# Sample attention values in four TensorE column groups: probabilities stationary, cache moving

## The reference

```python
def dilated_gather_decode(q, kv_new, kv_cache, dil, n_keys, slopes):
    ...
    s = (jnp.einsum('bthe,btkhe->bthk', q, kvg[:, :, :, 0]) * (ATT_DH ** -0.5)
         - slopes[:, None] * (dil * kk).astype(jnp.float32)[None, :])
    ...
    o = jnp.einsum('bthk,btkhe->bthe', p, kvg[:, :, :, 1]) / l[..., None]
```

## Time and profile before

| | us |
|---|---|
| median of three runs | 1918.61 |
| lowest and highest run | 1913.48, 1918.93 |
| the profiled execution, its own time | 1915.92 |
| span of the profiled execution | 1914.1 |
| TensorE matmul busy | 1828.6 (96%) |
| VectorE, ScalarE, GpSimd busy | 1039.6, 910.9, 773.9 |
| granted TensorE clock, mean over the span | 0.978 |

### The profile page before, as it was taken

The page is one execution under the profiler, slowest core; times in us unless marked ns, Lnnn a source line. Parts: engine busy times, 40 slices in busy tenths (PEclk is TensorE's granted clock), DMA queues, the critical chain, the costliest instruction groups (busy, mean ns, idle before and its releaser), DMA issues.

```text
span 1914.1 us, 32457 instructions
## 1 busy us (share of the span) xinstructions
PE 1828.6 (96%) x14108; PEld 1761.3 (92%) x14108; DVE 1039.6 (54%) x1120; ACT 910.9 (48%) x1064; POOL 773.9 (40%) x225
## 2 busy tenths in 40 slices
PE   8999999999979999999999979999999999899997
PEld 7999989999969999888989968999999999899997
DVE  4454555675386654455545463776254455557743
ACT  5555555444454435344444443443455565554443
POOL 4545434555215554321221201355354454455541
PEclk9999989999989999999999988999999999899999
DMA  8766854555435555845455522454667668545552
GB/s 269 260 222 245 296 177 154 186 180 166 129 111 172 181 168 187 238 144 160 140 160 141 159 71 68 131 176 161 209 219 265 225 240 289 187 133 176 176 182 84
DMA packets 306036, 346.33 MB, mean 181 GB/s; under 512 B 7847, under 2 KB 269479, under 8 KB 305887
## 3 DMA queue, kind: packets, MB, share of 16 engines
q1 hardware_dynamic: 257968, 260.36, 43.2%
q10 hardware_dynamic: 47927, 83.90, 12.5%
HBM read 299.66 MB, written 44.82 MB: 180 GB/s over the span
## 4 chain that ended last, share of the span: by engine, by line
PE 82%; DVE 9%; ACT 4%; issue 2%; DMA 1%; ACTq 1%; PEldq 0%; DVEq 0%
PE acc L1485 20%; PE acc L1486 20%; PE acc L1492 20%; PE mix L1625 2%; PE mix L1921 2%; PE mix L1883 1%; PE mix L1547 1%; PE acc L1513 1%; ACT w_hi L433 1%; PE acc L1514 1%; DVE w_lo L925 1%; PE acc L1519 1%; PE mix L1856 1%; PE mix L1637 1%; PE mix L1714 1%
## 5 line engine op out<-in xcount | busy, mean ns | idle before, releaser
L1392 POOL TENSOR_TENSOR w_lo<-raw,w_hi 128x2048 fp32r<-128x2048 f32 (+2 forms) x162 | 690.3, 4266 | 712.0 <-ACT w_hi L433 712.0
L1485 PE MATMUL acc<-g_hi,w_hi 128*128 128x264 f32 x2544 | 638.2, 289 | 8.7 <-DVE gate L1182 2.9
L1486 PE MATMUL acc<-g_lo,w_hi 128*128 128x264 f32 x2544 | 627.4, 284 | 0.0
L433 ACT ACTIVATE w_hi<-raw 128x2048 fp32r<-128x2048 f32 (+3 forms) x260 | 455.7, 1755 | 160.7 <-PE acc L1492 79.1
L925 DVE TENSOR_TENSOR w_lo<-raw,w_hi 128x2048 fp32r<-128x2048 f32 (+2 forms) x98 | 381.1, 3888 | 269.0 <-ACT w_hi L433 269.0
L1485 PEld LDWEIGHTS acc<-g_hi,w_hi 128*128 128x128 f32 x2544 | 478.3, 188 | 17.2 <-issue 12.2
L1486 PEld LDWEIGHTS acc<-g_lo,w_hi 128*128 128x128 f32 x2544 | 480.8, 189 | 1.3
L1492 PE MATMUL acc<-g_hi,w_lo 128*128 128x264 f32 x2544 | 343.8, 285 | 0.6 <-POOL w_lo L1392 0.6
L1492 PEld LDWEIGHTS acc<-g_hi,w_lo 128*128 128x128 f32 x2544 | 325.9, 188 | 2.3 <-POOL w_lo L1392 0.8
L1425 POOL TENSOR_TENSOR h_lo<-hid,h_hi 128x528 fp32r<-128x528 f32 x44 | 59.1, 1343 | 332.9 <-ACT h_hi L707 332.9
L1485 PE MATMUL acc<-h_hi,w_hi 128*128 128x264 f32 x664 | 164.1, 284 | 0.0
(11 more groups left out here) (238 smaller groups left out, 2460.1 us busy)
## 6 DMA issues: line engine op xcount, KB each, us to landing
raw<-in_w_ffn_in_dram SPq DMA_DIRECT2D x88, 1024.0 KB, 5.3
raw<-in_w_in_ret_dram SPq DMA_DIRECT2D x48, 1024.0 KB, 7.0
raw<-in_w_in_attn_dram SPq DMA_DIRECT2D x36, 1024.0 KB, 5.6
st<-in_state_ret_dram ACTq DMA_DIRECT2D x64, 512.0 KB, 6.7
out_dram<-st ACTq DMA_DIRECT2D x64, 512.0 KB, 6.2
raw<-in_w_ffn_out_dram SPq DMA_DIRECT2D x32, 768.0 KB, 4.8
raw<-in_w_ffn_out_dram SPq DMA_DIRECT2D x32, 640.0 KB, 4.9
raw<-in_w_out_ret_dram SPq DMA_DIRECT2D x16, 1024.0 KB, 7.5
```

What stands on the lines that cost most here:

```text
L433: A(w_hi[:, u % SPL, 0:size[u]], raw[:, u % RAW, 0:size[u]], ACT.Copy).then_inc(hi_split, 1)
L1392: TT(w_lo[:, u % SPL, 0:size[u]], raw[:, u % RAW, 0:size[u]], w_hi[:, u % SPL, 0:size[u]].bitcast(F32), ALU.subtract).then_inc(lo_by_pool, 1)
L1485: MM(out, wh, x_hi[:, ks[k], :], start=first and k == 0, stop=False)
L1486: MM(out, wh, x_lo[:, ks[k], :], start=False, stop=False)
```

## The change

At s = 7 all matmuls of the quad are done, with the operands swapped: the four columns of probabilities of a sample and block x are stationary (128 x 4) and the 256 values of the quad move (128 x 256). Sample b = 4 half + j goes to column group j of the array (`tile_position=(0, 32*j)`), with its result on PSUM partitions 32j to 32j+3 of bank 2, columns 256 half on. Half 0 is done in slot 0 and half 1 in slot 1. VectorE then copies the whole bank (128 x 512) to `dprod` in SBUF. At s = 8, in slot 0, TensorE turns four 128 x 128 blocks of `dprod` into bank 3, and nothing is done in slot 1. VectorE picks the wanted heads for both tiles with four copies of 64 partitions x 8.

```diff
@@ VectorE, decode_end @@
-                    if s >= 7:
-                        t = s - 7
-                        dve.wait_ge(dpv_done, 2 * q + t + 1)
+                    if s == 7:
+                        dve.wait_ge(dpv_done, 2 * q + 1)
+                        nc.vector.tensor_copy(dprod, mix[:, 2, :].rearrange("p (x n) -> p x n", x=2))\
+                            .then_inc(dpv_read, 1)
+                    if s == 8:
+                        dve.wait_ge(dpv_done, 2 * q + 2)
                         for half in range(2):
                             a = 64 * half
-                            src = mix[a:a + 64, 3, 320 + 32 * t:352 + 32 * t].rearrange("p (b h) -> p b h", h=4)
-                            ins = nc.vector.tensor_copy(y[a:a + 64, 2 * q + t, SEQ:T], src[:, :, 2 * t + half])
+                            src = mix[a:a + 64, 3, :].rearrange("p (g t j r) -> p g t j r", g=2, t=2, j=4)
+                            for t in range(2):
+                                ins = nc.vector.tensor_copy(
+                                    y[a:a + 64, 2 * q + t, SEQ:T].rearrange("p (g j) -> p g j", g=2),
+                                    src[:, :, t, :, 2 * t + half])
                         ins.then_inc(dpv_read, 1)
@@ TensorE, decode @@
-                    if s >= 7:
-                        t = s - 7
+                    if s == 7:
                         pe.wait_ge(dpt_ready, q + 1)
-                        for b in [4 * part + j for part in parts for j in range(4)]:
-                            out = mix[:, 3, 320 + 32 * t + 4 * b:324 + 32 * t + 4 * b]
+                        for half in parts:
                             for x in range(2):
-                                ins = MM(out, vc[:, b, x, t * P:(t + 1) * P], dPT[:, x, 4 * b:4 * b + 4],
-                                         start=(x == 0), stop=(x == 1))
+                                for j in range(4):
+                                    b = 4 * half + j
+                                    ins = MM(mix[32 * j:32 * j + 4, 2, half * UC:(half + 1) * UC],
+                                             dPT[:, x, 4 * b:4 * b + 4], vc[:, b, x, :],
+                                             start=(x == 0), stop=(x == 1), tile_position=(0, 32 * j))
                         if 1 in parts:
                             ins.then_inc(dpv_done, 1)
+                    if s == 8 and 0 in parts:
+                        pe.wait_ge(dpv_read, 2 * q + 1)
+                        for half in range(2):
+                            for t in range(2):
+                                at = (2 * half + t) * P
+                                ins = TR(mix[:, 3, at:at + P], dprod[:, half, t * P:(t + 1) * P], ident)
+                        ins.then_inc(dpv_done, 1)
```

## The result

The changed kernel takes 1893.06 us (median of four runs, 1892.65 to 1893.80) against 1916.30 us (1913.48 to 1918.93) for the kernel before, where a fourth run of 1914.00 us has joined the three that the forecast started from. The ratio is 0.9879 (95% interval 0.9861 to 0.9898): 23 us faster. The profiled execution has a span of 1891.2 us, 22.9 us less than the 1914.1 us before.

The account below looks back on a forecast made before the run. TensorE was taken to bound the kernel. 7.0 us saved in the three covered quads plus 4.5 in the last made 11.5, so 1918.6 us became a median forecast of 1907, range 1896 to 1923.

Parts of the forecast that it names:

- What bounds the kernel: Whole kernel: TensorE, busy for 96% of the span; in the first three quads its matmul costs are paid in full.
- what was removed: Value matmuls in all four quads: 256 go, 64 records per quad at 106 ns each, 6.8 us a quad.
- Gained and given back: Rival, chance 0.09: TensorE reaches later steps of a quad 2 us earlier and waits; about 1915 us, no change.
- The price of a record: New value matmuls at s = 7: 0.107 us a record, 1.7 us per part, two streams at a time.
- the shape change: Entering and leaving the column-group records at s = 7: 0.3 us per part, bounds 0 and twice that.
- The clock in the last quad: Last quad: granted clock 0.70 on average before; staying as before or full decides 1 or 8 us saved.
- The two walks: Last quad's steps added up twice: clock as before saves about 1.2 us, full clock about 8; middle 4.5 taken.
- Both signs: At s = 7, starts 0.05 to 0.08 us apart mean four streams; between 1152 and 1172, clock 1.0 means 8 us.
- low end: Whole kernel: four groups at the full clock, 9.8 + 10 us saved, giving 1896 us.
- The small terms: At s = 7 and 8: transposes 0.11 us apart, copy 0.69 us, covered waits free, no later weight loads.
- no overlap: Rival, chance 0.17: column groups at s = 7 don't overlap, 0.21 us a record; 1923 us, counted as no change.
- the waiting load: Rival, chance 0.08: at s = 7 each load waits for the running stream, 0.30 us a record; 1936 us.

## Why the prediction was wrong, point by point

**What bounds the kernel, and what was removed:** right. Sixteen old records cost 1.70 us, and the covered quads passed on what they gained: 4.3 us from the second quad to the third and 4.5 from the third to the last, against 6.8 - 2 x 1.07 - 0.45 = 4.2. "Gained and given back" didn't come about as a new wait. The second quad lost 3 us to the clock, which a kernel with the old code there lost too.

**The price of a record was the first failure.** The bounds used were 0.08 us (issue) and 0.30 us, the value 0.107 us (two streams at a time). The stream, 0.21 us, was right (0.216 measured). The number of streams was wrong: four run at once, and the forecast had two, because the step assumed that a record waiting for its group holds back the others. The lower bound was no bound: it took the distance of the two smallest records in the trace for what the issue allows, and 16 narrow records were issued in 0.34 us. With the shape change at 0.2 instead of 0.3 us, a part is 1.07 us instead of 2.0. Six parts in the covered quads: 6 x 0.93 = 5.6 us more than forecast.

**The clock in the last quad was the second.** The two walks gave 1.2 and about 8 us, and the text took 4.5 in the middle. It was the full clock, with the shorter parts on top: 8.7 us in the stretch and 1.9 after it, 10.6 instead of 4.5, 6.1 us more. Of the 8.7 us the clock is 4.7 (the old matmuls with 64 columns moving took 12.61 us), and the new records and steps are the other 4.0. Both signs that the forecast had named for the larger gain showed: starts 0.045 us apart, and the clock at 1.00. The evidence in the earlier trace rows pointed both ways, the clock falling during records with four moving columns in the last quad and not in the first; the forecast named it and then averaged.

**The sum:** 11.5 + 5.6 + 6.1 = 23.2 us, against 22.9 in the profile; the 3 us of the slow stretch in the second quad and the 2 us of the earlier start nearly cancel, and that is luck. The forecast of 1907 us also started from 1918.6 us, where the fourth run makes the median before 1916.3. The range missed because its low end, though it had four groups and the full clock, had them at 0.08 us a record, 1.3 + 0.3 = 1.6 us a part. Its terms don't quite add up either: at 1.6 us a part the covered quads save 9.5 us and not 9.8, and the 10 us for the last quad are in neither walk, which give 8 plus 2 x 0.4 = about 9. That moves the low end by 1.5 us at most and doesn't change the outcome.

**The small terms** held: transposes 0.11 us apart, copy 0.68 us, no wait behind it in the covered quads (0.38 us in the last), and no new wait for weights in TensorE's list. Four picks took 0.50 us instead of 0.66.

**The rivals:** no overlap is refuted by 0.97 against 3.54 us a part, the waiting load by the same rows. The kernel without groups, 1914 us, is what the first of them would have given. It was priced at 1923: 3.6 us of the difference is the kernel before, whose median beside it was 1915.0 and not 1918.6, and the rest is mostly the last quad, which kept the full clock.

## What to carry to other kernels

Where few columns move through a full stationary tile, the fill sets the price, not the work: 16 records took 1.70 us with four columns (902.56 to 904.26) and 1.73 with 64 (1151.46 to 1153.19). Swap the operands and spread the small side over column groups with equal shares: with 256 columns the step then lasted as long as the fullest group's records, plus 0.1 us, and the other order cost 0.03 us more. The swap without the groups gained next to nothing. A matmul that is busy but moves few columns can also cost the clock of what stands around it, 4.7 us in the last quad here; where a trace shows the half clock next to such records, price the change at the full clock and give that case its own weight instead of averaging. And a bound taken from the smallest example in a trace is an example, not a limit.

## What the runs showed of the hardware that was not expected

- Records for different column groups don't wait for each other: 16 records of 0.216 us in 0.97 us, and nearly the same (1.00 us) with four in a row to one group. With 64 columns 16 records took 0.34 us, with 16 columns 0.32.
- Moving 64 columns instead of four, at the same distance between records, kept the granted clock in the last quad at 1.0 where it had been 0.70 on average, and made the kernel 6 us faster.
- One wait of 2.46 us was followed by about 7 us at the half clock in the changed kernel (972 to 979) and in one with the old code there (976 to 983), and by none in the kernel before. The times of these kernels differ by up to 3 us on account of such stretches, which cover a gain of 1 or 2 us: two of the versions above gained in their own stretch and not in the median.
- VectorE's scaling between two SBUF tiles took 4.10 us beside GpSimd's work and 0.34 us without it; with its source in PSUM it took 0.47 us beside the same work.
